# A two-block sequence model on one core: input order, PSUM banks of the pooled chunks, denominators, and the tail's subtractions

## The reference, cut to what matters

```python
x = first_block(...)     # projections, three kinds of attention, gated merge, conv feed-forward, final norm
x = mlstm_pool_layer(x)  # layer "a"
x = mla_layer(x)         # layer "c"

# first block, where it starts: two inputs are normed, mem goes first
k, v = split(rms(mem, g_mem) @ w_mem_kv)
q_a, k_a, v_a, q_r, ... = split(rms(x, g_mix) @ w_in)

# layer "a": one head of the mLSTM (4 heads of 256), shown without chunks
s = (q @ k.T) * decay                 # causal, 256 x 256
num, den = s @ v, s.sum(-1)
h = num / max(abs(den), exp(-m))
ya = (headnorm(h * sigmoid(om)) + skip * xc) * silu(zm)
yb = (mix @ pool_w) * pool_scale * silu(zp)       # 4 groups of 256
x = x + concat(ya, yb) @ a_w_out

# layer "c": attention with 8 heads of 128 + 64 rotary columns, values of 128
o = softmax(mask(q @ k.T / sqrt(192))) @ v * silu(z)
x = x + o @ c_w_out
```

## Time and profile before

| | us |
|---|---|
| median of 3 runs | 833.51 |
| lowest and highest | 832.02, 834.57 |
| the profiled execution | 831.42 |
| its span, first to last instruction | 829.6 |
| TensorE busy | 801.0 (97%) |
| VectorE busy | 567.7 (68%) |
| ScalarE busy | 432.3 (52%) |
| GpSimd busy | 131.4 (16%) |
| mean granted TensorE clock | 0.988 |

### The profile page before, as it was taken

One profiled execution on the slowest core, in us unless ns is written; L12 is line 12 of the kernel. 1 busy time (PEld: TensorE's weight loads), 2 busy tenths in 40 slices (PEclk: granted clock), 3 DMA queues, 4 the chain that ended last, 5 costly groups with the idle time before them and its releaser, 6 DMA issues.

```text
span 829.6 us, 11993 instructions
## 1 busy us (share of the span) xinstructions
PE 801.0 (97%) x4640; PEld 698.8 (84%) x4640; DVE 567.7 (68%) x938; ACT 432.3 (52%) x585; POOL 131.4 (16%) x98
## 2 busy tenths in 40 slices
PE   8799999999999999999999999999999989998998
PEld 7588788888888899999988888998898868876766
DVE  5555566796468677878764495769864895896763
ACT  5745544344534475655643464645745245795441
POOL 0011650000000005454440000041410000042000
PEclk9899999999999999999999999999999999998999
DMA  9887433325455465554545544334655333743101
GB/s 342 323 286 258 152 124 134 142 109 172 145 191 203 168 245 192 200 171 186 196 162 201 202 153 170 135 127 167 231 183 190 107 109 115 283 162 143 51 1 51
DMA packets 23220, 142.78 MB, mean 172 GB/s; under 512 B 3548, under 2 KB 4456, under 8 KB 7040
## 3 DMA queue, kind: packets, MB, share of 16 engines
q1 hardware_dynamic: 20016, 134.51, 45.2%
q10 hardware_dynamic: 1776, 4.12, 1.3%
q0 software_dynamic: 1376, 3.43, 1.2%
HBM read 140.97 MB, written 2.64 MB: 173 GB/s over the span
## 4 chain that ended last, share of the span: by engine, by line
PE 77%; DVE 14%; ACT 4%; issue 2%; DMA 2%; SPq 0%; ACTq 0%; DVEq 0%
PE gemm L471 15%; PE gemm L472 15%; PE gemm L473 15%; PE gemm L477 8%; PE gemm L478 8%; PE gemm L479 8%; DVE wlo L1646 4%; DMA raw<-in_weights 2%; ACT whi L1148 2%; DVE xc L2165 2%; PE head L537 1%; PE head L727 1%; PE head L872 1%; PE head L871 1%; DVE rs_a L1656 1%
## 5 line engine op out<-in xcount | busy, mean ns | idle before, releaser
L1646 DVE TENSOR_TENSOR wlo<-raw,whi 128x2048 fp32r<-128x2048 f32 x122 | 282.1, 2314 | 119.9 <-ACT whi L1148 119.7
L1148 ACT CAST whi<-raw 128x2048 fp32r<-128x2048 f32 x122 | 232.6, 1906 | 216.9 <-PE gemm L473 122.3
L471 PE MATMUL gemm<-whi,x0hi 128*128 128x512 f32 (+2 forms) x400 | 158.7, 397 | 4.3 <-DVE x0lo L1833 2.6
L473 PE MATMUL gemm<-whi,x0lo 128*128 128x512 f32 (+2 forms) x400 | 154.9, 387 | 0.0
L472 PE MATMUL gemm<-wlo,x0hi 128*128 128x512 f32 (+2 forms) x400 | 154.9, 387 | 0.0
L477 PE MATMUL gemm<-x1hi,whi 128*128 128x256 f32 x400 | 114.5, 286 | 3.4 <-DVE om L2208 2.7
L478 PE MATMUL gemm<-x1lo,whi 128*128 128x256 f32 x400 | 113.8, 285 | 0.0
L479 PE MATMUL gemm<-x1hi,wlo 128*128 128x256 f32 x400 | 113.8, 284 | 0.0
L471 PEld LDWEIGHTS gemm<-whi,x0hi 128*128 128x128 f32 x400 | 76.0, 190 | 20.8 <-DVE x0lo L1833 3.3
L473 PEld LDWEIGHTS gemm<-whi,x0lo 128*128 128x128 f32 x400 | 75.9, 190 | 15.1
L472 PEld LDWEIGHTS gemm<-wlo,x0hi 128*128 128x128 f32 x400 | 76.1, 190 | 13.7
(11 more groups left out here) (345 smaller groups left out, 1356.4 us busy)
## 6 DMA issues: line engine op xcount, KB each, us to landing
raw<-in_weights SPq DMA_DIRECT2D x122, 1024.0 KB, 4.8
raw<-in_weights SPq DMA_DIRECT2D x4, 512.0 KB, 6.4
bias_rows<-bias_row POOLq DMA_DIRECT2D x1, 1536.0 KB, 15.0
memt<-in_memt SPq DMA_DIRECT2D x4, 256.0 KB, 5.3
tok<-in_mem SPq DMA_DIRECT2D x1, 1024.0 KB, 9.6
xt<-in_xt SPq DMA_DIRECT2D x1, 1024.0 KB, 12.2
xres<-in_x ACTq DMA_DIRECT2D x1, 1024.0 KB, 7.8
bias<-bias_rows POOLq DMA_DIRECT2D x8, 128.0 KB, 4.3
```

Of the source, the lines that this page charges most:

```text
L471: mm(o, xh, wh, start=start, stop=False)
L473: return mm(o, xl, wh, start=False, stop=stop)
L1148: nc.scalar.copy(whi[:, p % RING, :], raw[:, p % RING, :]).then_inc(s_hi, 1)
L1646: V.tensor_tensor(wlo[:, p % RING, :], raw[:, p % RING, :], whi[:, p % RING, :].bitcast(F32), ALU.subtract).then_inc(s_lo, 1)
```

## The change

Five parts, all in the program of one core:

1. **Start.** SP loads `tok` after half of piece 1, then piece 3, half of `xt`, piece 4, the other half of `xt`, piece 5, and then `ident`. ScalarE waits for the half of `xt` that it reads. ScalarE starts the load of `xres` in step 2, after split 4.
2. **Pool stage, wq, wk.** The third and fourth chunk of these phases go into the second bank of their pair; TensorE waits for chunk c - 4 for them, and for all four of `wk`. In the step of `pool` both engines split the piece after the last mix copy and subtraction, not ahead of them. The emptying of a pooled chunk waits for the gate `zp` by a semaphore.
3. **Denominators.** `v_ml` gets a 257th column of ones per head, set by GpSimd once the `zm` phase is multiplied; the six matmul instructions at L788 go. Token tile 0 of a weighed head is in A[3], tile 1 in A[0]; VectorE gates them in two instructions and copies the two denominators in two. GpSimd's skip multiplications stand behind the setting of the ones.
4. **Head steps.** From step e = 4 on `ml_dve` comes ahead of `split(p + 2)`.
5. **Tail.** VectorE splits in odd steps the piece that the next step needs, and no longer ahead of the loop; ScalarE copies the turned rotary parts ahead of the exponential.

```diff
-LATE_SPLIT = (p0("up"), p0("xp") - 1, ...
+LATE_SPLIT = (p0("pool"), p0("up"), p0("xp") - 1, ...
...
-            [("u_up", [P, 2, 2, S], F32)], [("v_ml", [P, T, D], F32)])
+            [("u_up", [P, 2, 2, S], F32)], [("v_ml", [P, T, ML_H, S + 1], F32)])
...
+        FOUR = [c0(name) + n for name in ("pool", "wq", "wk") for n in (2, 3)]
+
         def bank(c, t=0):
-            return G[2 * (c % 2) + t]
+            return G[2 * (c % 2) + (1 if c in FOUR else t)]
...
+        def ml_bank(t):
+            return A[3] if t == 0 else A[0]
...
-            sp.wait_ge(s_piece[0], 16)
+            def next_piece(p):
+                sp.wait_ge(s_lo, p - RING + 1)
+                sp.dma_start(raw[:, p % RING, :], ins["weights"][p]).then_inc(s_piece[p % RING], 16)
+
+            sp.wait_ge(s_half_piece[1], 16)
             sp.dma_start(tok[:, 12:14, :, :].rearrange("p a b c -> p (a b c)"), ins["mem"]).then_inc(s_mem, 16)
-            sp.dma_start(xt[:, :, :].rearrange("p k s -> p (k s)"), ins["xt"]).then_inc(s_xt, 16)
+            next_piece(3)
+            sp.dma_start(xt[:, 0:4, :].rearrange("p k s -> p (k s)"), ins["xt"][:, 0:4 * S]).then_inc(s_xt[0], 16)
+            next_piece(4)
+            sp.dma_start(xt[:, 4:8, :].rearrange("p k s -> p (k s)"), ins["xt"][:, 4 * S:8 * S]).then_inc(s_xt[1], 16)
+            next_piece(5)
             sp.dma_start(ident[:, :], ins["ident"]).then_inc(s_ident, 16)
...
                 for t in range(T):
                     for i, st in enumerate(range(t + 1)):
                         col = t * P if st == 0 else S
-                        mm(A[3][:, t * S:t * S + S], prob[:, h % 2, col:col + P],
-                           v_ml[:, st, h * S:h * S + S], start=i == 0, stop=st == t)
-                for t in range(T):
-                    for i, st in enumerate(range(t + 1)):
-                        col = t * P if st == 0 else S
-                        last = mm(A[0][:, 400 + t:401 + t], prob[:, h % 2, col:col + P], ones[:, 0:1],
-                                  start=i == 0, stop=st == t)
+                        last = mm(ml_bank(t)[:, 0:S + 1], prob[:, h % 2, col:col + P],
+                                  v_ml[:, st, h, :], start=i == 0, stop=st == t)
...
                 if e == 0:
+                    pe.wait_ge(s_vones, 1)
...
-                        chunk_free(pe, c - 2)
+                        chunk_free(pe, c - (2 if g < 2 and name != "wk" else 4))
...
-                        act.wait_ge(s_xt, 16)
+                        act.wait_ge(s_xt[i // 2], 16)
...
+                    if e < 2:
+                        for k in (2 * e, 2 * e + 1):
+                            act.wait_ge(s_lpt, k + 1)
+                            nc.scalar.copy(pe_q[:, k, :], A[3 - k % 2][:, :]).then_inc(s_ltp, 1)
                     if 1 <= e < MLA_H + 1:
...
                     if e in (2, 6):
                         z_tanh((e - 2) // 4)
-                    if e < 2:
-                        for k in (2 * e, 2 * e + 1):
-                            act.wait_ge(s_lpt, k + 1)
-                            nc.scalar.copy(pe_q[:, k, :], A[3 - k % 2][:, :]).then_inc(s_ltp, 1)
...
-                if p == 1:
+                if p == 2:
                     act.dma_start(xres[:, :, :].rearrange("p t d -> p (t d)"), ins["x"]).then_inc(s_x, 16)
...
+                if p == p0("pool"):
+                    split(p + 2)
...
-                    V.scalar_tensor_tensor(hm[h % 2], om[:, :, h * S:h * S + S], 1.0,
-                                           A[3][:, :].rearrange("p (t d) -> p t d", t=T),
-                                           ALU.add, ALU.mult).then_inc(s_hm, 1)
+                    for t in range(T):
+                        i = V.scalar_tensor_tensor(hm[h % 2][:, t, :], om[:, t, h * S:h * S + S], 1.0,
+                                                   ml_bank(t)[:, 0:S], ALU.add, ALU.mult)
+                    i.then_inc(s_hm, 1)
...
-                    order(V.tensor_copy(rsum[:, :], A[0][:, 400:402]))
+                    for t in range(T):
+                        i = V.tensor_copy(rsum[:, t:t + 1], ml_bank(t)[:, S:S + 1])
+                    order(i)
...
-                split(Z0 + 2)
                 for e in range(14):
...
-                    if e % 2 == 0:
-                        split(piece_of(e) + 2)
+                    if e % 2:
+                        split(piece_of(e + 1))
...
                     elif name == "pool":
+                        dve.wait_ge(s_zd, n + 1)
...
                 head_dve(p)
+                if p >= ML0 + ML_H:
+                    ml_dve(p)
                 if p not in LATE_SPLIT:
                     split(p + 2)
-                ml_dve(p)
+                if p < ML0 + ML_H:
+                    ml_dve(p)
                 if p < ML0 + 6:
                     ya_lo(p)
...
+                if p == p0("pool"):
+                    split(p + 2)
...
+            pool.wait_ge(s_mm, p0("zm") + 4)
+            Q.memset(v_ml[:, :, :, S:S + 1], 1.0).then_inc(s_vones, 1)
             pool.wait_ge(s_xclo, 4)
```

More of the change, by code:

```diff
@@ L144 @@
 REL_STEP = 4
-LATE_SPLIT = (p0("up"), p0("xp") - 1, p0("xp"), p0("xp") + 1, p0("cu") - 1, p0("cu"), p0("cu") + 1)
+LATE_SPLIT = (p0("pool"), p0("up"), p0("xp") - 1, p0("xp"), p0("xp") + 1, p0("cu") - 1, p0("cu"), p0("cu") + 1)
 JOBS = [head_at(n) for n in range(MOBA0, MEM0 + MEM_H)]
@@ L286, in program @@
         s_memt = [s_memt] + [sem(f"mem_columns_loaded_{i}") for i in range(2, 5)]
+        s_xt = [s_xt, sem("x_columns_loaded_2")]
         s_gain, s_onehot = sem("gains_loaded"), sem("onehot_loaded")
@@ L322, in program @@
         s_hm = sem("ml_h_gated")
+        s_vones = sem("value_ones_ready")
         s_md = sem("max_rows_moved")
@@ L441, in _ @@
             sp.dma_start(raw[:, 2, :], ins["weights"][2]).then_inc(s_piece[2], 16)
-            sp.wait_ge(s_piece[0], 16)
+            def next_piece(p):
+                sp.wait_ge(s_lo, p - RING + 1)
+                sp.dma_start(raw[:, p % RING, :], ins["weights"][p]).then_inc(s_piece[p % RING], 16)
+            sp.wait_ge(s_half_piece[1], 16)
             sp.dma_start(tok[:, 12:14, :, :].rearrange("p a b c -> p (a b c)"), ins["mem"]).then_inc(s_mem, 16)
-            sp.dma_start(xt[:, :, :].rearrange("p k s -> p (k s)"), ins["xt"]).then_inc(s_xt, 16)
+            next_piece(3)
[3 more added lines that the diff above has]
+            next_piece(5)
             sp.dma_start(ident[:, :], ins["ident"]).then_inc(s_ident, 16)
             rounds = NPIECES // RING
-            with sp.Fori(1, rounds) as r:
+            with sp.Fori(2, rounds) as r:
                 for j in range(RING):
@@ L1518, in empty @@
                         for t in range(T):
-                            done = nc.scalar.copy(v_ml[:, t, n * 512:n * 512 + 512], bank(c, t)[:, :])
+                            done = nc.scalar.copy(v_ml[:, t, 2 * n:2 * n + 2, 0:S],
+                                                  bank(c, t)[:, :].rearrange("p (h d) -> p h d", d=S))
                     elif name in ("wq", "wk"):
```

## The result

The changed kernel runs in 819.1 us (median of 4 runs, 818.7 to 819.2) against 832.8 (832.0 to 834.6): ratio 0.984, 95% interval 0.982 to 0.985. Forecast were 820.7, within 816 to 827. The profiled execution took 819.2 (span 817.4); the sum had 818.6. So 12.2 us came off the span where the sum had 12.8. The terms have to be read one by one.

What follows compares the result with a forecast made beforehand. TensorE, busy 801 of 829.6 us, was taken to bound the kernel, so only its waits, low-clock stretches or removed matmuls could pay. Terms 2.7 + 1.5 + 0.6 + 0.2 + 7.8 = 12.8 gave median 820.7, range 816 to 827.

Steps and rivals of the forecast that it cites:

- Start: Start: piece 3 lands 2.7 us earlier, shifting the chain to the x0lo subtractions; TensorE waits about 4.1; gain 2.7.
- the lower bound: Start: gain 1.6 us less if the longer x0lo wait costs a second slow clock stretch.
- The rival that the x columns become last: Start: x columns, in halves behind pieces 3 and 4, land last, so no gain there; 823.4 us, chance 0.08.
- Pooled chunks: Pool stage: four banks let chunks follow at once; a 2.2 us wait replaces 2.7, one chunk later; gain 1.5.
- 2.1 us kept it, 2.7 lost it, so I take the middle: Pool stage: whether the clock falls behind the new 2.2 us wait; gain 1.5 between bounds 0.7 and 2.3.
- wq and wk: wq step: chunks 3 and 4 no longer wait for ScalarE; gain 0.6 us.
- Denominators: mLSTM heads: the ones column saves TensorE 2.4 us, but VectorE sets these steps, so TensorE waits the rest; gain nothing.
- Head-step reorder: Last head steps: gating ahead of the split; second ya subtraction stays behind the split; gain 0.2 us, bounds -1.6 and 4.0.
- The rival at 0.12: Head steps: the reorder pays in full, ya subtraction not the next bound; 4.0 instead of 0.2, 816.9 us; chance 0.12.
- Tail: Tail: 2.7 us wait and 3.4 of slow clock go (6.1), wait at 799 goes (2.1), last piece -0.4; gain 7.8.
- with the copies ahead of the exponential both end by 757.4: Tail: ScalarE's pe_q copies and exponential both finish by 757.4, before TensorE's unit ends at 758.5.
- The rival that the stretches come anyway: Whole kernel: slow clock stretches follow the chip's state, not the waits; sum 8.6, 824.9 us; chance 0.10.

Runs made afterwards that it cites:

- experiment 8: Changed kernel with the scaling and subtractions of the x columns one step earlier on ScalarE and VectorE: 817.4 us, ratio 0.983 to the kernel before.
- experiment 12: Changed kernel with pooled multiplications and ya subtractions ahead of VectorE's split, x columns split a step earlier, and ScalarE's old tail order: 809.3 us, ratio 0.972.
- experiment 5: Changed kernel with VectorE's eight pooled multiplications ahead of its piece's subtraction in the pool step: 815.6 us, ratio 0.980 to the kernel before.
- experiment 6: Changed kernel with the pool step's splits early again on both engines, the four banks kept: 817.3 us, ratio 0.982 to the kernel before.
- experiment 4: Changed kernel with VectorE's gating behind its split again in the last two head steps: 818.3 us.
- experiment 7: Changed kernel with the ya subtractions of two head steps also ahead of VectorE's split: 815.0 us, ratio 0.979 to the kernel before.
- experiment 2: Kernel before with only ScalarE's pe_q copies moved ahead of the exponential in the tail: 830.7 us, ratio 0.998.
- experiment 10: Kernel before with only the start's transfers in the new order: 828.9 us, ratio 0.996.
- experiment 9: The changed kernel run once more as it is: 819.5 us (816.5 to 819.9).

## Why the prediction was right, and where not

**Start (2.7, got 2.4 to 2.8).** Right in every step: piece 3's landing set the chain, everything behind shifted by it, the new wait is 4.15. The 0.3 missing in the changed kernel's trace is clock. The low stretch now begins inside the wait and lasts until 40.2, costing 2.1 (half of the 2.1 us worked up to 38, and 0.28 x 4 behind) where 1.7 went before. The longer wait thus had its longer stretch, as the lower bound feared, but half of that stretch is waited away. The rival that the x columns become last is false for the wait as it stands (experiment 8 starts on them 5 us earlier), and comes true where they are wanted at 26.6, in experiment 12.

**Pooled chunks (1.5, got 0.8).** The waiting was right, 2.0 at the place named. What failed is the step "2.1 us kept it, 2.7 lost it, so I take the middle". The clock fell, and the middle of two outcomes is an outcome that no single execution has. More was wrong behind it: the length of a wait does not settle it in this range (below). That the late split itself was the cost, experiments 5 and 6 show; I had costed the wait and not asked whether the move that makes it was needed.

**wq and wk (0.6, got 1.2).** TensorE's 0.58 for q_ml went as forecast, and with it a shorter wait (0.1 at 631 in wk). The rest is what surrounds a wait. Matmuls of 256 columns last 0.28 but start 0.12 apart; around a wait this overlap is lost, and the first one behind it lasts longer (0.35 at 540.66). So a wait of TensorE costs more than its length: that of 0.58 cost 0.85, and in the tail that of 0.37 for the last piece cost 0.7 (the table's last row). No experiment takes this part of the change alone; the account is read from the two traces.

**Denominators (0, got 0.7).** The mechanism was right: VectorE sets these steps, and most of the saving is waited. Two sizes were off. "0.2 to 0.3 per head" measured 0.12, and "of the 2.4 only the first head's 0.6 moves that start" came out near 0.7. The 257th column costs nothing that shows.

**Head-step reorder (0.2).** Right: the same 5.0 us of waits in either order, and the next bound was the subtraction that the prediction named. The rival at 0.12, that it pays in full, is refuted by experiment 4 and made true by 7, with 4.1.

**Tail (6.1 + 2.1 - 0.4, got 5.5 + 2.1 - 0.7).** Right in place and size. But the step "with the copies ahead of the exponential both end by 757.4" failed. The exponential ended at 753.6 in the changed kernel, which is 758.8 in the old kernel's time, 1.4 later than that. VectorE's half brings everything alone, and ScalarE's reorder takes 0.3 to 0.5 back, since it puts the copies and the table load of 1.28 between the bias and the exponential. The load had been in the trace all the time, hidden under ScalarE's 5.9 us of waiting; I priced the instructions that move and not one that a moved instruction drags along. The Trainium skill (ScalarE: Activation LUTs, "Step-by-step: what each stage is for", table-load gate) has the load placed right before the function that needs it. The three kernels shown agree: in each it is the instruction ahead of the exponential.

**The clock.** The rival that the stretches come anyway is wrong as it was put: where a wait was taken away (at 759 by the change, before the xm phase and the second aout piece by experiments 5 and 7) the stretch went too, and no trace has one away from a wait while TensorE has work. But the rule by which I priced it, that it follows waits of 2.4 and spares 2.1, is refuted: 1.6 and 2.08 lost the clock, 3.3 kept it. The rule of the Trainium skill that was weighed (TensorE: Matmul & The Clock Gate, HAM oscillation) does not fit either: by it only the wait of 4.15 would cost clock in the changed kernel, and its waits of 2.0 and 2.2 did. What the traces allow as the price of a wait of 1.6 to 3.3 us is its length and 0, 1.7 or 3.4 more. Counted over all 14 traces (the kernels before and after and the twelve experiments), waits of the start left out:

| wait of TensorE | us | traces with it | with a low stretch behind it |
|---|---|---|---|
| head steps, xc, the first | 1.6 | 9 | 0 |
| tail, prob (experiment 2) | 1.6 | 1 | 1 |
| first xm chunk, om | 2.0 | 7 | 6 |
| tail, olo | 2.1 | 3 | 2 |
| second aout gemm, x1lo (a wait of 1.2 just ahead) | 2.2 | 7 | 7 |
| third pooled chunk, om | 2.7 | 4 | 4 |
| tail, pe_q | 2.7 | 2 | 2 |
| last head's transposes, xc | 3.3 to 3.4 | 5 | 4 |

Longer waits lose the clock more often, but the length does not decide it. What does stays open: no run placed one wait at chosen times.

## What to carry to other kernels

When a split or another bulk operation stands ahead of something small on a busy engine, ask for every small operation behind it who waits for it. Three times here (the tail, the pool stage, the last head steps) 2 to 3 us of TensorE's time hung on one or two subtractions of 2.3 that stood ahead of small work. In the head steps it was not enough to move the first small operation ahead; the gain came when the next one moved too.

Before crediting two edits with one gain, find out whether one is enough, and look at what an edit moves silently, a table load above all.

Take a wait's price in clock as a range and never as a middle value, and read a difference of 1 to 3 us between two kernels beside each run's granted clock before giving it to an edit.

## What the hardware showed that was not expected

- Equal waits, different clock: behind 2.07 and 2.08 us it was 1.00 (kernel before) and 0.50 (experiment 10); behind 3.33 and 3.32 us 0.57 (kernel before) and 1.00 (experiment 2); behind 2.02 us 0.57 in the changed kernel and 1.00 in experiment 4.
- The clock can fall within the wait: in the changed kernel it is 0.50 over 34 to 38, of which TensorE waits the first half.
- The changed kernel, in the five runs of experiment 9, took 816.5 once and 819.4 to 819.9 four times, at a mean granted clock of 0.996 and 0.991 to 0.992.
- A pair of 128x256 operations from PSUM costs 0.74 in one form and 0.86 or 0.87 in another on VectorE (gating and xc update, both scalar_tensor_tensor).
